# Ten products of constants left out around the routing of a mixture of experts

## What is computed

```python
def moe(h, w_router, b_router, w_gate, b_gate, w_up, b_up, w_down, b_down):
    logits = jnp.dot(h, w_router) + b_router
    top_logit, top_idx = lax.top_k(logits, TOP_K)          # 4 of 32 experts
    gates = jax.nn.softmax(top_logit, axis=-1)
    ...                                                    # tokens sorted by expert
    def expert_block(args):
        xb, e = args
        g = jnp.minimum(xb @ w_gate[e] + b_gate[e], SWIGLU_LIMIT)
        u = jnp.clip(xb @ w_up[e] + b_up[e], -SWIGLU_LIMIT, SWIGLU_LIMIT)
        act = g * jax.nn.sigmoid(SWIGLU_ALPHA * g) * (u + 1)
        return act @ w_down[e] + b_down[e]
    ...                                                    # weighted by the gates and summed per token
```

## Time and profile before

| | |
|---|---|
| median of three runs | 1881.03 us (1880.22 to 1882.22) |
| profiled execution | 1879.11 us |
| its span, first to last instruction | 1877.3 us |
| granted TensorE clock, mean | 0.996 |
| TensorE products busy | 97% of the span |
| TensorE weight loads busy | 53% |
| VectorE busy | 27% |
| ScalarE busy | 19% |
| moved from and to memory | 558.43 MB, mean 297 GB/s |

### The profile page before, as it was taken

The page is one execution under the profiler, slowest core; times in us unless marked ns, Lnnn a source line. Parts: engine busy times, 40 slices in busy tenths (PEclk is TensorE's granted clock), DMA queues, the critical chain, the costliest instruction groups (busy, mean ns, idle before and its releaser), DMA issues. The chain is left out here.

```text
span 1877.3 us, 21793 instructions
## 1 busy us (share of the span) xinstructions
PE 1824.7 (97%) x8661; PEld 998.6 (53%) x8662; DVE 505.1 (27%) x1093; ACT 348.3 (19%) x688; POOL 10.9 (1%) x14
## 2 busy tenths in 40 slices
PE   6999899999999999999999999999999999999998
PEld 5757533333333333333333336768885466788743
DVE  1754411111011111011111104542025443211355
ACT  3221411111111111111111113332000032220001
POOL 0000000000000000000000000000000000000001
PEclk9999899999999999999999999999999999999999
DMA  9986599999999999999999999423355443134252
GB/s 401 324 184 276 207 416 430 431 432 432 431 431 431 433 431 431 431 431 432 431 431 430 432 429 328 155 105 105 135 176 177 146 174 135 45 135 158 86 170 102
DMA packets 101218, 558.43 MB, mean 297 GB/s; under 512 B 16936, under 2 KB 33805, under 8 KB 74413
## 3 DMA queue, kind: packets, MB, share of 16 engines
q1 hardware_dynamic: 98612, 553.06, 72.4%
q10 hardware_dynamic: 2554, 4.63, 1.9%
HBM read 552.43 MB, written 5.23 MB: 297 GB/s over the span
## 5 line engine op out<-in xcount | busy, mean ns | idle before, releaser
L1362 PE MATMUL ps<-ring,xs 128*64 128x512 f32 x2112 | 466.9, 593 | 8.5 <-DMA ring<-in_w_up 4.7
L1362 PEld LDWEIGHTS ps<-ring,xs 128*64 128x64 f32 x2112 | 151.1, 137 | 312.7 <-issue 293.9
L1416 PE MATMUL ps<-ring,actT 128*64 128x512 f32 x1056 | 233.9, 595 | 0.0
L2149 PE MATMUL ps<-hT,ring 128*128 128x256 f32 x1024 | 222.0, 379 | 0.2 <-ACT hT L1614 0.2
L2149 PEld LDWEIGHTS ps<-hT,ring 128*128 128x128 f32 x1024 | 194.3, 190 | 27.0 <-ACT hT L1614 0.6
L2174 PE MATMUL ps<-ring 128*128 128x512 f32 x448 | 192.8, 592 | 0.0
L1416 PEld LDWEIGHTS ps<-ring,actT 128*64 128x64 f32 x1056 | 73.1, 137 | 158.5 <-issue 131.7
L1489 DVE TENSOR_SCALAR hT<-ps 128x512 f32<-128x512 f32 x33 | 22.8, 692 | 448.0 <-PE ps L1362 448.0
L2174 PEld LDWEIGHTS ps<-ring 128*128 128x128 f32 x448 | 85.0, 190 | 105.8 <-issue 105.7
L1937 PE MATMUL ps<-hT,ring 128*128 128x256 f32 x512 | 117.9, 383 | 4.3 <-ACT hT L1614 2.9
L1937 PEld LDWEIGHTS ps<-hT,ring 128*128 128x128 f32 x512 | 94.7, 190 | 23.2 <-issue 5.9
(11 more groups left out here) (434 smaller groups left out, 1548.1 us busy)
## 6 DMA issues: line engine op xcount, KB each, us to landing
ring<-in_w_up SPq DMA_DIRECT2D x64, 2048.0 KB, 23.2
ring<-in_w_down SPq DMA_DIRECT2D x64, 2048.0 KB, 24.2
ring<-in_w_gate SPq DMA_DIRECT2D x64, 2048.0 KB, 22.7
ring<-in_mlp_w SPq DMA_DIRECT2D x16, 2048.0 KB, 7.7
ring<-in_mlp_w SPq DMA_DIRECT2D x32, 1024.0 KB, 5.3
ring<-in_w_mod SPq DMA_DIRECT2D x8, 2048.0 KB, 15.4
ring<-in_odd_w_in SPq DMA_DIRECT2D x6, 2048.0 KB, 7.7
ring<-in_w_mod SPq DMA_DIRECT2D x8, 1024.0 KB, 14.1
```

The source lines that it names most:

```text
L1362: mm = pe.matmul(ps[SLOTS * half:SLOTS * (half + 1), bank, :], xs[:, c % 4, c // 4 * SLOTS:(c // 4 + 1) * SLOTS], weights(v, 8 * part + c) ...
L1416: mm = pe.matmul(ps[SLOTS * half:SLOTS * (half + 1), Y, :], actT[:, f % 4, f // 4 * SLOTS:(f // 4 + 1) * SLOTS], weights(v, 16 + f)[:, hal ...
L2149: mm = pe.matmul(ps[:, bank + f // 2, (f % 2) * SEQ:(f % 2 + 1) * SEQ], mlp_w1[layer][g % 2][:, c, f * P:(f + 1) * P], hT[:, c, :], start= ...
```

## The change

Four calls of `keep_busy` go: four products between the logits and the ranks, four between the ranks and the pass counts, one behind the spreading at the end of the block, and one in the second block between the turn of the first rows and the load of the number of passes. Nothing else is changed, moved or added, and every wait stays.

```diff
@@ -710,7 +710,6 @@
             mm.then_inc(lg_ps, 1)
 
-            keep_busy(m, pe, 4, 4)
             pe.wait_ge(picked, 8)
@@ -719,7 +718,6 @@
             pe.matmul(ps[0:EXPERTS, 5, 1:2], cst(m, "etri", EXPERTS), ones[0:EXPERTS, 0:1], start=True, stop=True).then_inc(rank_ps, 1)
-            keep_busy(m, pe, 3, 4, SEQ)
             pe.wait_ge(more_chain, 5)
@@ -746,7 +744,6 @@
             pe.wait_ge(turned_sb, 4)
             begin(4)
-            keep_busy(m, pe, 0, 1)
             pe.wait_ge(m.brows_in, 32)
 
@@ -1379,7 +1376,6 @@
             pe.wait_ge(xrow_sb, 1)
             turn_x()
-            keep_busy(m, pe, Y, 1)
             n = passes(pe)
             pe.wait_ge(bdown_in, 32)
```

## The result

Over twenty executions of each kernel, the changed kernel's median is 1881.91 us (1880.22 to 1885.39) and that of the kernel before 1879.35 us (1877.72 to 1882.82): a ratio of 1.0014, 95% interval [1.0008, 1.0020], or +2.6 us. That is slower, clear of noise, and inside the 0.2% that the prediction called no change. The forecast was +0.5 us. The three executions of before that the prediction had (median 1881.03) lay 1.7 us above the median of the twenty, so 1881.5 was close to 1881.91 partly by luck: the forecast difference was too small by 2.1 us. Put on the median of the twenty, the same range would run from 1877.6 to 1882.8 us and hold the result still.

What follows compares the result with a forecast made beforehand. TensorE, then the weight stream, bounds the kernel. Ranks 0, spreading +1.50, third product -0.59, gather -0.43 and expansion 0 sum to +0.48 us; on the median of 1881.03 that is 1881.5 us, range 1879.2 to 1884.4.

Steps and rivals of the forecast that it cites:

- What bounds the kernel: Expert stage: TensorE bounds it, then the weight stream; any shift of the first expansion's start reaches the end one for one.
- Ranks: cost 0: Ahead of the ranks: eight weight loads take 1.7 us instead of 0.9, hidden behind VectorE's other work; cost 0.
- Pass counts and spreading: From pass counts through the twelve spreading records: half clock delays VectorE's read of the spread keys by 1.50 us.
- Third product: Behind the spreading: removal alone gives 0.59 us; with late spreading VectorE ends the block and the gather starts at 222.77.
- The gather's return of 0.43: In the gather: full clock returns at about 225.4, so the later gather wins back 0.43 us.
- the 0 for the expansion: Ahead of the first expansion: it stays 2.61 us behind its turns and runs at full clock; cost 0.
- the first rival: Around gather and first expansion: the clock falls once more or rises late, slower by 1.2 to 2.2 us; chance 0.25.
- the third rival: First pass of the experts: half clock lasts deep into it, to 235.7 or beyond, slower by over 3.76 us; chance 0.05.
- the signs that I had named against the forecast: Full clock within 212 to 218, gather before 221.9, expansion within 2.3 us of its turns, or second low stretch behind 229.
- The fourth product: Ahead of the first expansion: removing it costs 0, as loop-bound loading runs beside it; bounds 0 and -0.43 us.
- The rule of the Trainium skill: Ahead of the first expansion: transposes don't count as clock activity, so the turns there would not help hold the clock.

Runs made afterwards that it cites:

- the first four experiments: The kernel before without the ranks' four products, without the pass counts' four, without both groups, without both single products: 1880.09, 1880.47, 1880.27, 1880.55 us, each against 1879.21.

## Why the prediction was right, and where it wasn't

**What bounds the kernel: right.** The prediction said that what happens to the first expansion goes to the end one for one. The second gather and the end moved by +3.95 and +4.1 us after the change, by +0.8 and +0.8 without both groups, by -0.95 and -1.0 with all waits filled. Over all thirteen traces of other kernels than before, the two differ by 0.7 us at most.

**Ranks: cost 0, right.** The rank loads took 1.78 us (1.7 predicted) and ended at 213.75; VectorE read the ranks at 215.22. VectorE was 0.42 us late at the masks (210.86 against 210.44 in the earlier trace rows), and that isn't the change's: 0.2 us were there already when the logits (L710) started, and 0.2 came from the logits, which took 0.97 instead of 0.75 us because the clock fell at 208.3 in both traces. Both lie ahead of the first place that was changed.

**Pass counts and spreading: right.** VectorE's read of the spread keys was predicted 1.50 later and came 1.85 later (221.95 against 220.10), of which 0.42 is the delay just named: 1.43 for the step itself. The twelve spreading records stand 0.21 apart, as expected.

**Third product: right.** VectorE ends the block. The gather was predicted at 222.77 and came at 223.15, which is the same 0.4. Of its +1.29, then, the change made 0.87, where 0.91 was predicted.

**The gather's return of 0.43, and the 0 for the expansion: the step that failed.** I let the clock rise at 225.4, where it had risen before. In the profiled execution the gather ran wholly at half clock (3.68 us again, but from later on), the clock didn't rise behind it either, and it stayed at half over biases, turns and 5.0 us of the first expansion. The second gather's +3.95 adds up so: +1.29 for the gather's start, 0 in the gather where -0.43 stood, +0.18 at the start of the expansion and +2.48 in the expansion, where 0 stood for both. The price was right: 5.0 us of dense products at half clock cost 2.48, the 0.5 for each microsecond that the prediction had. What was wrong is how long the half clock lasts. I had put a moment of rising that isn't fixed at a fixed place in time.

The text named the other outcome as the first rival, "rises late", at +1.2 to +2.2 with a chance of 0.25; the median of +2.6 lies just above its end. The profiled execution is the third rival, over 3.76 if the low stretch lasts to 235.7, which had 0.05: it lasted to 235.6, and the span is 4.1 us longer, 0.4 of which lie ahead of the change. The mechanism of the loss was on the list; its size and its chance were too small. Of the signs that I had named against the forecast two came: half clock behind 229, as the continuation of the first low stretch and not as a second one, and an expansion within 2.3 us of its turns (1.90), though not because the fourth product was on the path, as shown below.

**Why the clock didn't rise: not settled.** The late gather alone isn't it. Without the first group, without the second and without both, the gather starts at 223.40, 223.44 and 223.15, as late as after the change, and the clock is back at 225.3, 226.7 and 225.7. What all three have and the changed kernel hasn't is the two single products. All eight traces with the third product at its full width, the one behind the spreading, have full clock again 1.9 to 4.2 us after the gather's start. Of the six without it only one does, after 4.4 us (that without both singles); the other five take 8.8 to 12.5 us, into the expansion. I had priced this product by its own time, -0.59, and gave its clock no term. But the mean clocks over all executions show no more than a small part for it: leaving it out costs 0.0004 when all else stays, 0.0011 when the fourth is gone and 0.0001 when the groups are gone. So the pattern of one trace per kernel is a lead and not a proof.

**The fourth product: 0 for its own time, right; its effect too small.** The expansion started at 228.15 with one product and with four. It also isn't bound to the turns, as I had it (2.61 us behind them). By the traces it follows the later of two things. Where the turns run at full clock it starts 2.9 to 3.1 us behind the end of ScalarE's copy of the rows: 2.94 in before (226.16, as 225.58 + 0.58), and 2.92 and 2.95 in the two kernels that have both groups and no fourth product, so that product cost nothing. Where the turns run at half clock it starts 0.15 us behind the end of the copy of the turned rows: after the change at 230.57 behind 230.42 (229.84 + 0.58). At half clock biases and turns put off that copy's end by 1.3 us against the copy of the rows. All but 0.2 of it hid, because in before the expansion started 1.25 us behind the end of that copy (227.85).

As a holder of the clock the fourth product has the clearest trace: with both groups kept, the first expansion loses its clock for 3.3 us when it is gone, in both traces. In mean clock, leaving it out costs 0.0003 when all else stays, 0.0010 when the third is gone and 0.0012 when all others are. In that last case it seems to make about 1.6 of the 2.6 us. The medians without it are not clear of noise by themselves, and the last figure rests on overlapping intervals.

**The rule of the Trainium skill.** By the Trainium skill, "TensorE: Matmul & The Clock Gate", Part 4, the turns wouldn't count towards activity. Two kinds of run agree with it as far as they go. With one-column products the clock stays at half over the turns (from 228.10). Without the fourth it falls 0.3 and 0.6 us into the expansion, behind a stretch of biases, turns and idle time. But no run here had turns alone, so the rule isn't tested.

**What stays open.** How the loss divides over the four places: the first group alone gave +0.9, the second +1.3, both +1.1, the third product +0.3 and the fourth +0.6, all within the same interval. Why the late rise goes with the third product. And why filling all waits won 0.8 us instead of 3: in the trace the fall moved behind the routing, onto the gather, but whether it does so in most executions a single trace doesn't say.

## What to carry to other kernels

A product that computes nothing can be worth its place if it holds the clock for those behind it, and its own time then tells nothing: ask what the real products around it would take at half clock, and what the first dense stretch behind would lose until the clock is back. Don't leave the moment of a rise or a fall where the old trace has it: it can change with what TensorE does around it, and it moves where the instructions are the same, so take several executions' clocks, not one trace. Give every filler two prices, its own time and what the clock does without it, also the one whose own time is a gain. And a filler in a wait is hidden only at the clock that it was measured at; four of them here went from 1.99 to 3.78 us and onto the path.

## What the runs showed of the hardware that I had not expected

With the same instructions up to 220 us, the clock fell at 208.3 in the trace of before and at 217.8 in that without the third product. In the 33 executions beside the first four experiments the kernel before itself took 1877.6 to 1883.3 us at mean clocks of 0.993 to 0.998. And after the change the half clock held for 27.3 us, from 208.3 to 235.6, of which the records call TensorE busy for 21.05:

```profile
208.30:235.60 27.30, 21.05 (x83) 11.50 (x84) 10.83 (x53) 8.00 (x17) 0.00 (x0) 0.50 0.24 83
```

This is a line of the table of stretches, columns as in the earlier trace rows. A narrow product and a turn count as busy there as a wide one does.
